# The opening stage's loads and transposes placed inside the first FFN, and two layers written out

## The reference

```
def first_block(x, ...):
    for l in range(2):
        x = layer_norm(ALPHA * x + 0.5 * swiglu(x, ffn1_w_gate[l], ffn1_w_up[l], ffn1_w_down[l]), ln1_g[l], ln1_b[l])
        y = hybrid_mixer(x, w_in[l], ...)                 # projection, attention, pooling, w_out[l]
        x = layer_norm(ALPHA * x + y, ln2_g[l], ln2_b[l])
        x = layer_norm(ALPHA * x + 0.5 * swiglu(x, ffn2_w_gate[l], ffn2_w_up[l], ffn2_w_down[l]), ln3_g[l], ln3_b[l])
    return x

def swiglu(x, w_gate, w_up, w_down):                      # hidden width 2816 = 22 tiles of 128
    return (silu(x @ w_gate) * (x @ w_up)) @ w_down

mod[l] = silu(c) @ w_mod[l] + b_mod[l]                    # second block's; computed ahead, inside the first block's FFNs
```

## Time and profile before

| | |
|---|---|
| median of 3 runs | 2526.01 us (2521.97 to 2526.62) |
| profiled execution | 2526.09 us |
| its span, first to last instruction | 2524.4 us |
| mean granted TensorE clock | 0.951 |
| TensorE busy, weight loads | 2301.0 us (91%), 1895.4 us (75%) |
| VectorE, ScalarE, GpSimd busy | 58%, 45%, 5% |
| DMA | 350 MB, mean 139 GB/s |

### The profile page before, as it was taken

How to read it: one execution, slowest core, us unless ns; L and a number is a source line. 1 busy time by engine, 2 the same in 40 slices (tenths; PEclk the granted TensorE clock), 3 DMA queues, 4 the chain that set the end, 5 groups by cost and what they waited for, 6 DMA issues and landing times. The chain is left out here.

```text
span 2524.4 us, 38180 instructions
## 1 busy us (share of the span) xinstructions
PE 2301.0 (91%) x14476; PEld 1895.4 (75%) x14476; DVE 1459.5 (58%) x2330; ACT 1132.6 (45%) x1910; POOL 124.0 (5%) x159
## 2 busy tenths in 40 slices
PE   6998999998999998999779997869999979977998
PEld 6786877877887777877448886658888768855886
DVE  6565257666666346666545675375455554436886
ACT  3444254444444245444266664344333444434654
POOL 1000001001000001000001222000000000001000
PEclk9999999998999999999899998989999979988999
DMA  7786135875786414885112110144433443304663
GB/s 228 251 264 208 41 116 154 265 248 153 237 265 221 107 68 143 249 249 167 44 42 80 47 60 2 34 127 115 125 102 114 133 104 81 93 3 141 190 184 91
DMA packets 394393, 350.05 MB, mean 139 GB/s; under 512 B 24484, under 2 KB 357656, under 8 KB 393752
## 3 DMA queue, kind: packets, MB, share of 16 engines
q1 hardware_dynamic: 384180, 297.63, 40.6%
q10 hardware_dynamic: 10084, 50.66, 5.1%
HBM read 347.20 MB, written 1.05 MB: 138 GB/s over the span
## 5 line engine op out<-in xcount | busy, mean ns | idle before, releaser
L556 PE MATMUL ps<-x_hi_lo,gu_hi 128*128 128x512 f32 x1680 | 425.1, 395 | 8.0 <-DVE gu_sum L721 8.0
L556 PEld LDWEIGHTS ps<-x_hi_lo,gu_hi 128*128 128x128 f32 x1680 | 306.8, 189 | 87.5 <-issue 26.4
L721 DVE TENSOR_REDUCE gu_sum<-ps 128x256 f32<-128x512 f32 x220 | 151.2, 689 | 264.3 <-PE ps L558 264.3
L633 ACT ACTIVATE gu_hi<-w_gu 128x1024 fp32r<-128x1024 f32 x220 | 230.0, 1055 | 105.4 <-DVE gu_sum L721 60.3
L704 DVE TENSOR_TENSOR gu_lo<-w_gu,gu_hi 128x1024 fp32r<-128x1024 f32 x220 | 265.8, 1243 | 4.2 <-ACT gu_hi L633 4.2
L558 PEld LDWEIGHTS ps<-x_hi_lo,gu_lo 128*128 128x128 f32 x1680 | 230.5, 191 | 17.0
L558 PE MATMUL ps<-x_hi_lo,gu_lo 128*128 128x256 f32 x1680 | 235.4, 283 | 0.0
L585 PE MATMUL ps<-dn_hi,h_hi 128*128 128x512 f32 x440 | 173.6, 395 | 3.0 <-DVE h_lo L744 3.0
L585 PE MATMUL ps<-dn_lo,h_hi 128*128 128x512 f32 x440 | 173.1, 393 | 0.0
L585 PE MATMUL ps<-dn_hi,h_lo 128*128 128x512 f32 x440 | 171.9, 391 | 0.0
L644 ACT ACTIVATE silu<-gu_sum 128x256 f32<-128x256 f32 x88 | 36.7, 417 | 271.4 <-DVE gu_sum L721 271.4
(11 more groups left out here) (418 smaller groups left out, 4915.9 us busy)
## 6 DMA issues: line engine op xcount, KB each, us to landing
w_gu<-in_ffn_w_up SPq DMA_DIRECT2D x178, 512.0 KB, 6.1
w_dn<-in_ffn_w_down SPq DMA_DIRECT2D x134, 512.0 KB, 3.7
w_mod<-in_w_mod ACTq DMA_DIRECT2D x64, 768.0 KB, 7.0
w_gu<-in_ffn_w_gate SPq DMA_DIRECT2D x90, 512.0 KB, 4.9
odd_w<-in_odd_w_qkv SPq DMA_DIRECT2D x24, 512.0 KB, 5.1
w_gu<-in_ffn_w_down SPq DMA_DIRECT2D x11, 1024.0 KB, 5.0
hgrn_w<-in_even_w_in SPq DMA_DIRECT2D x20, 512.0 KB, 4.0
wo<-in_w_out SPq DMA_DIRECT2D x2, 4096.0 KB, 14.0
```

The source lines that it names most:

```text
L556: pe.matmul(gu(a), gu_hi[n][:, a, f, :], x_both[:, f, :, :], start=(f == 0), stop=False, skip_group_check=True)
L633: act.activation(gu_hi[n][:, a, :, :], wgu[n][:, a, :, :], ACT.Copy).then_inc(s["w_hi"], 1)
L721: dve.reduce_sum(c[n][:, a, :], gu(a).rearrange("p h t -> p t h"), AX.X).then_inc(s["c_ready"], 1)
```

## The change

- `params_phase` is gone. A class `Begin` does its work inside the first FFN of layer 0. SP: identity and x first, then the two weight tiles, then the six other constants, the 18 parameter loads, the context (into the buffer of x), then the usual reloads. TensorE turns x (16 transposes) and waits for all constants before the products with alpha; it turns the parameter rows after tile 0, the context in two halves after tiles 1 and 2. VectorE copies x at once, and constants, parameters and context at the end of steps 0 to 2. ScalarE makes the padded c in step 1 and issues the first two loads of the modulation's weights in step 2.
- The layer loop is written out in Python; both `settle` calls are gone, and the last FFN of the first block loads no tiles ahead.
- In every `ffn_phase`: `x_lo` moves from GpSimd to VectorE, behind `lo_gu` of tile 0; `lo_dn` of tiles 0 and 1 move into step 0, one behind the sums, one at its end.
- `mixer1_project`: the turn of the position tables moves behind the token products.

```diff
+    def load_tokens(self, sp, s):
+        sp.dma_start(self.k.ident[:, :], self.w["c_ident"]).then_inc(s["ident_in"], 16)
+        for tt in range(TT):
+            sp.dma_start(self.x_rows[:, tt, :], self.w["x"][0, tt * P:(tt + 1) * P, :]).then_inc(s["x_in"], 16)
+    def load_rest(self, sp, s):
+        for dst, src in self.consts:
+            sp.dma_start(dst, src).then_inc(s["const_in"], 16)
+        sp.wait_ge(s["rows_zeroed"], 1)
+        for name, tile, r in self.VECTORS:
...
+            sp.dma_start(rows[r:r + src.shape[0], tile, :], src).then_inc(s["rows_in"], 16)
...
+        sp.wait_ge(s["x_turned"], FT // 2)
+        for tt in range(TT):
+            sp.dma_start(self.x_rows[:, tt, :], w["ctx_2"][0, tt * P:(tt + 1) * P, :]).then_inc(s["ctx_in"], 16)
+    def turn_x(self, pe, s):
...
+        pe.wait_ge(s["const_in"], 16 * len(self.consts))
+    def turn_rest(self, pe, s, step):
+        if step == 0:
+            pe.wait_ge(s["rows_in"], 16 * self.N_ROWS)
...
+        if step in (1, 2):
+            if step == 1:
+                pe.wait_ge(s["par_used"], 2)
+                pe.wait_ge(s["ctx_in"], 16 * TT)
+            else:
+                pe.wait_ge(s["ctx_used"], 2)
...
+    def keep_rest(self, dve, s, step):
+        if step == 0:
+            dve.wait_ge(s["const_in"], 16 * len(self.consts))
+            dve.tensor_copy(k.ident_r[:, :], k.ident[:, :])
+            dve.tensor_copy(k.causal_r[:, :, :], self.causal[:, :].unsqueeze(1).broadcast_to([P, 2, P])).then_inc(s["rounded"], 1)
+            dve.wait_ge(s["par_turned"], 1)
+            dve.tensor_copy(k.par[:, 0:512], k.ps[:, 6, :]).then_inc(s["par_used"], 1)
+            dve.tensor_copy(k.par[:, 512:PAR_TILES * P], k.ps[:, 7, 0:(PAR_TILES - 4) * P]).then_inc(s["par_used"], 1)
...
-                for f in range(FT):
-                    pool.wait_ge(s["x_hi"], f + 1)
-                    pool.tensor_tensor(x_lo[:, f, :], src(f), x_hi[:, f, :].bitcast(F32), ALU.subtract).then_inc(s["x_lo"], 1)
...
+                    if fixed == 0:
+                        lo_dn(0, 5)
...
+                    if fixed == 0:
+                        lo_dn(1, 6)
+                    if begin and fixed is not None:
+                        begin.keep_rest(dve, s, fixed)
...
-                for n in range(2):
-                    lo_dn(n, n + 5)
+                    if n == 0:
+                        dve.wait_ge(s["x_hi"], FT)
+                        for f in range(FT):
+                            dve.tensor_tensor(x_lo[:, f, :], src(f), x_hi[:, f, :].bitcast(F32), ALU.subtract).then_inc(s["x_lo"], 1)
...
-        params_phase(nc, k, w, first_loads(tiles, *ffn_weights(1, 0)))
-        settle(nc)
-        with nc.Fori(0, DEPTH) as l:
-            def norm(n):
+        for l in range(DEPTH):
+            def norm(n, l=l):
...
-                      ahead=first_loads(tiles, *ffn_weights(1, l * -1 + 1)), reloads=True)
-            settle(nc)
+                      ahead=first_loads(tiles, *ffn_weights(1, l + 1)) if l + 1 < DEPTH else (), reloads=l + 1 < DEPTH)
```

More of the change, by code:

```diff
@@ L473, in ffn_phase @@
+def ffn_phase(nc, k, w_gate, w_up, w_down, src, ln=None, conv=None, post=None, mod=None, loaded=None, ahead=(), reloads=False, begin=None):
     names = ["gu0_in", "gu1_in", "dn0_in", "dn1_in", "x_hi", "x_lo", "w_hi", "gate0_split", "gu_split", "dn_split", "gu_done", "c_ready", "mid_ready",
@@ L529, in load_dn @@
                     sp.dma_start(wdn[n][:, :], w_down[i]).then_inc(dn_in[n], 16)
+                if begin:
+                    begin.load_tokens(sp, s)
                 for n in range(2):
-                    if loaded:
+                    if loaded and not begin:
                         sp.sem_inc(gu_in[n], 32)
@@ L642, in step @@
                     act.wait_ge(s["c_ready"], t * 2 + 1)
+                    if begin and fixed is not None:
+                        begin.pad_c(act, s, fixed)
+                    if begin and fixed == 2:
+                        for half in range(2):
+                            load_mod(0, half)
                     if conv is None:
@@ L673, in load_mod @@
                     act.dma_start(wm[:, half, :, :].rearrange("p j n -> p (j n)"), mod[0](f, half)).then_inc(s[f"wm{half}_in"], 16)
-                if mod:
+                if mod and not begin:
                     for half in range(2):
@@ L690, in _ @@
             def _(pool):
-                for f in range(FT):
-                    pool.wait_ge(s["x_hi"], f + 1)
-                    pool.tensor_tensor(x_lo[:, f, :], src(f), x_hi[:, f, :].bitcast(F32), ALU.subtract).then_inc(s["x_lo"], 1)
+                if begin:
+                    begin.clear(pool, s)
                 if mod:
@@ L1216, in project @@
                     return last
-                pe.wait_ge(s["pos_in"], 32)
-                for n in range(2):
-                    last = pe.transpose(k.ps[0:HD, 7, n * CBLK:(n + 1) * CBLK], pos_rows[:, n, :], k.ident[0:CBLK, 0:CBLK])
-                last.then_inc(s["pos_turned"], 1)
                 for tt in range(TT):
@@ L1231, in _ @@
                     last.then_inc(s["tok_done"], 1)
+                pe.wait_ge(s["pos_in"], 32)
+                for n in range(2):
+                    last = pe.transpose(k.ps[0:HD, 7, n * CBLK:(n + 1) * CBLK], pos_rows[:, n, :], k.ident[0:CBLK, 0:CBLK])
+                last.then_inc(s["pos_turned"], 1)
                 for n in range(4):
```

159 lines of the change are left out of this document (87 added, 72 removed), and 6 rows, old and new, of tables (VECTORS, vectors).

## The result

| | forecast | measured |
|---|---|---|
| changed kernel, median | 2500.4 us (2493 to 2511) | 2490.66 us of 4 runs (2487.86 to 2493.23) |
| kernel before, same comparison | | 2526.32 us of 4 runs (2521.97 to 2529.13) |
| ratio | 0.990 | 0.986, 95% interval 0.9841 to 0.9879 |
| gain | 25.7 us | 35.7 us |

The profiled execution took 2489.22 us, with a span of 2487.4 against 2524.4; so it is 37.0 us whose whereabouts can be read, 11.3 more than the sum.

The account below looks back on a forecast made before the run. TensorE is busy throughout the FFN hidden-tile loop, so only its standstills or lower-clock time can be won. Terms 5.0 + 7.3 + 5.4 + 2.4 + 5.0 + 0.6 = 25.7; 2526.1 - 25.7 = 2500.4 us, range 2493 to 2511.

Parts of the forecast that it names:

- three signs of being wrong: Casts taking 5 us with GpSimd silent, TensorE waiting for parameter rows or context, or a loop turn above 18.3 us.
- part B: Second FFNs of both layers: faster casts and subtractions moved from before VectorE's sum end TensorE's wait; 3.65 us each, 7.3 us.
- D: FFN of the second block: casts run ahead of TensorE, which reaches tile 1 sooner; 2.4 us, bounds 0 and 3.3.
- Part E: Mixer projection: token products no longer wait for the position rows; 2.7 us in layer 0, 2.3 in layer 1, 5.0 us.
- A, opening: Start of the first FFN: reordered loads and parameter work inside it bring tile 2 from 46.48 to 40.4; net 5.0 us.
- Rival 2: Opening held by the one queue, constants and 18 small loads behind 3.1 MB: A gives 2.0, total 2503.4 us; chance 0.12.
- C, first FFN of layer 1: Start of layer 1: 3.8 us of the layer loop's jump goes, tile 1 at 620.4 against 625.84; 5.4 us.
- Rival 3: Idle time at the layer loop's jump remains as start-up of new code: 3.8 us back, 2504.2 us; chance 0.06.
- F: End of layer 1: ScalarE's idle time falls from 1.35 to 0.77 us; 0.6 us.
- Rival 4: Slower: duplicated FFN loops of layer 1 stall at each jump back, 14 x 3.2 = 45 us, 2545 us; chance 0.03.
- Rival 1, slow casts: VectorE's casts at FFN starts stay at about 5 us: gain 15.8 us, total 2510.3 us; chance 0.13.
- A at 7, clock gains everywhere: More than forecast: the opening gives 7 us and the clock gains everywhere; chance 0.04.

## Why the prediction was wrong

The direction, the places and nearly all the mechanisms were right, and none of the three signs of being wrong showed; the step that failed is the price of a standstill. It had 3.2 us of faster products where the profile has 18.2, beside 22.5 us of waits where it has 18.8. Some of the 18.2 is luck of the one profiled execution, as said below, but the gain is not: five more executions of the changed kernel were 36.9 us shorter by mean span. In part B I gave 1.6 us to the clock, in D I counted slow products, and everywhere else I priced a removed wait at its own length and took the durations around it from the trace as they stood. The alpha products stood there at 5.29 and 5.44 us; the same trace has 32 of them at 3.81:

```profile
950.32 3.81 PE L1092 MATMUL ps<-alpha,x_T 128*128 128x128 f32 x32 [0.73 <-PEq L207]
```

Part E even says what would happen "if the clock rises no earlier", and gives no value to its rising earlier, or to its not falling at all.

- **A, opening: 5.0 forecast, 5.8 in its stage.** Alpha at 17.93 (17.3), end of tile 0 near 29.1 (28.8), tile 2 at 39.34 (40.4), the turns 0.93 and 1.03 (0.9 and 1.1). Rival 2 had 2.0 for it and is out for the landmark; how much of the whole time it is stays between 2.3 and 5.3. Of the 5.8 in the stage, 3.6 are there with the old opening too: they come from the FFN's edit, whose share A had taken in when it left out the idle 2.12 us, and from the missing barrier.
- **B, second FFNs: 3.65 each.** Casts 1.72 (1.5 and up to 1.2 on top), VectorE's sum in time, idle time 0.44 at tile 1, slow products gone: as told. To tile 1 it is 3.6 us less, but the 3.6 is made up otherwise: about 1.1 of it comes from the alpha products, 5.44 to 3.81, which I had taken at the speed of the earlier trace rows, and hangs on the execution; the 1.6 of the products behind tile 1 come on top. Stage less jump: 8.4 - 3.8 = 4.6.
- **C, first FFN of layer 1: 5.4.** The jump gave 3.8 as forecast (idle 0.31). The rest gave 3.6, not 1.6: I set the start to tile 1 at 11.5 and a hand-over, after part B, and that stretch itself held slow alpha products; it is 10.00. Rival 3, that the idle time would remain, fell with the written-out layers alone.
- **D, second block: 2.4 forecast, 3.9 in the stage.** TensorE reaches tile 1 8.58 us after it begins (2281.58 to 2290.16); I had 9.7, and before it was 12.5. Its first sixteen products take 3.53 (forecast 3.6), but the next 2.08, not 3.6, and the wait for the sum at tile 1 is 1.23, not the 0.2 and 0.4 that I had for a hand-over and the late dn_lo. That the casts no longer set the pace held; the step that failed is again a run of products set at the lower clock.
- **E, mixers: 5.0 forecast, 10.0 in the profiled execution and 11.7 where the edit was alone.** The mis-sized term: idle 4.2, as forecast within 0.8, and products 7.4 in the single edit, 4.7 of them behind the wait. Of the 10.0, 1.5 us is luck: the layer norm's transposes in layer 1, ahead of the edit, took 3.60 us before and 2.08 after. Of the 11.3 us that the sum lacked, 5 are here.
- **F: 0.6.** ScalarE's idle time went from 1.35 to 0.68.
- **Edits at nothing.** The longer program costs nothing that can be seen: a loop turn of layer 1 takes 18.28 us (one modulation product at 665.61, the next at 683.89), as in layer 0 before. Rival 4, and with it the case of a slower kernel, is out. The Trainium skill's sentence that a taken branch may stall ("Runtime: NRT & Kernel Launch", section "Instruction fetch mechanics") fits the long jump back, 4.08 against 0.80 us, though no run shows that it was the fetching of code; the short jumps show no price.
- **Rival 1, slow casts:** out, by 1.72 against 4.96, shown with nothing else changed.
- **The range** took its upper gain from "A at 7, clock gains everywhere" and gave it a chance of 0.04. The kernel before had some 70 us at the lower clock ahead of the second block, 55 of them outside the attention stages, nearly all at phase starts and layer norms; after, 10 of the 55 are left. Half of them gone, at 0.27 us each (the slope above) to 0.5 (what a product at half speed loses), would have been 7 to 14 us. The dips and the slow products stood in the trace of before, and the case should have had a term of its own and not 0.04.

## What to carry to other kernels

A standstill of TensorE costs its length and, in many executions, slow products behind it; where a wait of 2 to 4 us stands at a phase start, read the granted clock of the window after it, and compare the same products at both levels before pricing its removal. Where two things hold back the same point (here slow casts and the order of VectorE's queue, or slow casts and slow alpha products), neither edit alone shows the gain: price them together and test them together. And where a wait can't be removed, some useless transposes in it can be cheaper than leaving TensorE idle. Count them at the lower clock, so that they still end before the wait does, and look for the standstill ahead of the one that you see: filling one alone gave nothing here.

## What the runs showed of the hardware

- The same 632 instructions of a mixer took TensorE 73.53 us at clock 1.00 and 76.0 to 78.2 at a mean of 0.94 to 0.96. With the standstill of 2.0 us ahead of a layer norm's sixteen transposes open, they were slow (2.6 to 3.6 instead of 2.08 us) at 30 of 72 layer norms; with it filled, down to 0.7 us, at none of 12.
- The 32 alpha products behind the layer loop's jump back took 5.8 to 6.8 us in seven of seven profiles, and 3.81 without the jump in seven of seven. The first 32 token products behind a standstill of 3.8 to 5.0 us took 10.6 to 12.2 us, and 9.17 to 9.20 at the full clock.
- Of one kernel the number of dips varies from run to run, and with it the span, by 0.27 us for each us at 1.2 GHz. Most of the spread of the kernel before (spans of 2518 to 2531 us) goes with it.
- VectorE's eight casts of 256 columns took 4.96 us beside GpSimd's subtractions on the same tile and 1.7 without them.
- The jump back of the layer loop held VectorE for 4.08 us, with nearly no data moving; a barrier alone held it for 0.80 and an ordinary phase start for 0.31.
